# Interleaved stationary columns and a reversed stream in a three-pass matmul kernel

## What is computed

```python
h = rms_norm(x, norm1_g)
z = h @ w_in                                   # pool part, q, k, v, forget gates
x = x + concat([pool_mixer(...), forgetting_attention(...)]) @ w_out
h = rms_norm(x, norm2_g)
q = h @ w_query                                # 8 heads x 2 x 128
# top 16 of 128 keys twice, top 16 of the 256 sums: 128 experts of 16384 for each frame
a = gelu(einsum('thkd,td->thk', expert_u[idx], h))
x = x + einsum('thk,thkd->td', gates * a, expert_v[idx])
```

## Time and profile before

| | us |
|---|---|
| median of 3 runs | 1440.59 (1440.06 to 1440.88) |
| profiled execution, own time | 1441.41 |
| profiled execution, span | 1439.4 |
| PE busy | 1431.6 |
| PE, loads of the stationary | 1277.2 |
| DVE busy | 1133.4 |
| POOL busy | 979.8 |
| ACT busy | 574.4 |

### The profile page before, as it was taken

How to read it: one execution, slowest core, us unless ns; L and a number is a source line. 1 busy time by engine, 2 the same in 40 slices (tenths; PEclk the granted TensorE clock), 3 DMA queues, 4 the chain that set the end, 5 groups by cost and what they waited for, 6 DMA issues and landing times.

```text
span 1439.4 us, 20447 instructions
## 1 busy us (share of the span) xinstructions
PE 1431.6 (99%) x7551; PEld 1277.2 (89%) x7551; DVE 1133.4 (79%) x1876; ACT 574.4 (40%) x799; POOL 979.8 (68%) x533
## 2 busy tenths in 40 slices
PE   9999999999999999999999999999999999999998
PEld 7766798899999999999999999888888888888887
DVE  6678551769999999699999995498777777777775
ACT  5775453333333333444444444333333333333332
POOL 3421544346888788866766675599887888878883
PEclk9999999999999999999999999999999999999999
DMA  6221332235778888989999986998888888888883
GB/s 227 103 89 45 103 113 100 89 100 184 251 262 268 273 272 273 348 281 364 355 360 355 372 296 230 371 383 340 346 346 346 327 326 345 344 341 328 331 302 117
DMA packets 122293, 381.57 MB, mean 265 GB/s; under 512 B 11768, under 2 KB 28280, under 8 KB 122240
## 3 DMA queue, kind: packets, MB, share of 16 engines
q1 hardware_dynamic: 70384, 202.69, 39.5%
q0 software_dynamic: 36864, 134.23, 25.3%
q10 hardware_dynamic: 14992, 44.06, 7.8%
HBM read 336.89 MB, written 44.06 MB: 265 GB/s over the span
## 4 chain that ended last, share of the span: by engine, by line
PE 95%; DVE 2%; DMA 1%; ACT 1%; issue 0%; SPq 0%; DVEq 0%
PE bank L748 28%; PE bank L749 28%; PE bank L750 28%; PE bank L1004 6%; PE bank L936 1%; DMA wf<-a_dram 1%; PE bank L884 1%; PE bank L907 0%; PE wide L896 0%; DVE pad L1235 0%; PE bank L815 0%; PE wide L815 0%; PE bank L826 0%; PE bank L822 0%; PE wide L822 0%
## 5 line engine op out<-in xcount | busy, mean ns | idle before, releaser
L484 POOL TENSOR_TENSOR wl<-raw,wh 128x1024 fp32r<-128x1024 f32 x208 | 507.7, 2442 | 277.7 <-ACT wh L514 275.1
L748 PE MATMUL bank<-hh,wh 128*128 128x384 f32 (+1 forms) x1184 | 416.2, 352 | 0.2 <-DVE hl L1251 0.2
L749 PE MATMUL bank<-hl,wh 128*128 128x384 f32 (+1 forms) x1184 | 406.4, 343 | 0.0
L750 PE MATMUL bank<-hh,wl 128*128 128x384 f32 (+1 forms) x1184 | 406.4, 343 | 0.0
L748 PE MATMUL bank<-wh,Wh 128*128 128x512 f32 x768 | 299.0, 389 | 0.7 <-DVE Wl L1458 0.7
L750 PE MATMUL bank<-wh,Wl 128*128 128x512 f32 x768 | 298.8, 389 | 0.0
L749 PE MATMUL bank<-wl,Wh 128*128 128x512 f32 x768 | 298.8, 389 | 0.0
L514 ACT ACTIVATE wh<-raw 128x1024 fp32r<-128x1024 f32 (+1 forms) x217 | 227.8, 1050 | 141.4 <-PE bank L750 136.4
L748 PEld LDWEIGHTS bank<-hh,wh 128*128 128x128 f32 x1184 | 222.8, 188 | 7.9 <-DVE hl L1251 0.6
L749 PEld LDWEIGHTS bank<-hl,wh 128*128 128x128 f32 x1184 | 222.8, 188 | 7.1 <-issue 0.2
L750 PEld LDWEIGHTS bank<-hh,wl 128*128 128x128 f32 x1184 | 222.3, 188 | 7.6
(11 more groups left out here) (200 smaller groups left out, 1628.6 us busy)
## 6 DMA issues: line engine op xcount, KB each, us to landing
raw<-uT_dram SPq DMA_DIRECT2D x128, 512.0 KB
xraw<-v_dram SPq DMA_DIRECT2D x72, 512.0 KB, 8.5
raw<-v_dram SPq DMA_DIRECT2D x56, 512.0 KB, 9.1
a_dram<-act_a ACTq DMA_DIRECT2D x64, 384.0 KB
wf<-a_dram SPq DMA_DIRECT2D x32, 768.0 KB, 6.8
raw<-wst_dram SPq DMA_DIRECT2D x40, 512.0 KB
gates_dram<-gbuf ACTq DMA_DIRECT2D x32, 512.0 KB
gt<-gates_dram SPq DMA_DIRECT2D x32, 512.0 KB, 4.0
```

Of the source, the lines that this page charges most:

```text
L484: pool.tensor_tensor(wl[:, n % SPLIT, :], raw_of(n), wh[:, n % SPLIT, :].bitcast(F32), ALU.subtract).then_inc(w_lo, 1)
L748: pe.matmul(dst, ah, bh, start=start, stop=False)
L749: pe.matmul(dst, ah, bl, start=False, stop=False)
L750: return pe.matmul(dst, al, bh, start=False, stop=stop)
```

## The change

It has two parts. First, wherever a stationary operand is read from a tile by `project` or `quad`, two neighbouring chunks of the contraction (k = 0 and 1, 2 and 3, ...) are now stored in turn: element 0 of the one, element 0 of the other, element 1 of the one, and so on. A load reads every second column, 128 of 256, and starts at column 0 or 1 of the pair. For the tiles that come from memory the host stores them so (`in_pairs`), with transfers of the same size; for `Wh` and `Wl` ACT and DVE write, and DVE also reads, with a step of two (`by_chunk`). The values and forget tiles stay as they were. Second, in the downs alone the streamed operand and the PSUM bank are both given with a step of -1 (`backwards`), so the columns stream from the last to the first and arrive in their old places. Number, order, waits and sizes of all instructions and transfers are the same on every engine; the two splits L728 and L1458 now have 2 x 2 x 384 instead of 1536 elements a partition.

```diff
+        def in_pairs(w):
+            return w[:, :, :].rearrange("p q t -> p (q t)")
+        def by_chunk(w):
+            return in_pairs(w).rearrange("p (a t c) -> p a c t", a=QUAD // 2, c=2)
+        def pairs_of(w):
+            return w[:, :, :].rearrange("p (a c) t -> p a c t", c=2)
...
-                act.activation(Wh[q % 2][:, :, :], wf[q % LOADS][:, :, :], ACT.Copy).then_inc(W_hi, 1)
+                act.activation(by_chunk(Wh[q % 2]), pairs_of(wf[q % LOADS]), ACT.Copy).then_inc(W_hi, 1)
...
+            def backwards(columns):
+                return columns[:, ::-1]
...
-                    done = three(dst, wh[:, s, k * P:(k + 1) * P], wl[:, s, k * P:(k + 1) * P],
+                    first_column = k // 2 * 2 * P + k % 2
+                    columns = slice(first_column, first_column + 2 * P - 1, 2)
+                    done = three(dst, wh[:, s, columns], wl[:, s, columns],
...
-                            at, d = slice(b * P, (b + 1) * P), slice(half * T, (half + 1) * T)
-                            done = three(bank[2 * b + half][:, :], Wh[s][:, c, at], Wl[s][:, c, at],
-                                         wh[:, static % SPLIT, d], wl[:, static % SPLIT, d], False, end)
+                            first_column = c // 2 * 2 * DT + 2 * P * b + c % 2
+                            at, d = slice(first_column, first_column + 2 * P - 1, 2), slice(half * T, (half + 1) * T)
+                            done = three(backwards(bank[2 * b + half][:, :]), in_pairs(Wh[s])[:, at], in_pairs(Wl[s])[:, at],
+                                         backwards(wh[:, static % SPLIT, d]), backwards(wl[:, static % SPLIT, d]), False, end)
...
-                dve.tensor_tensor(Wl[q % 2][:, :, :], wf[q % LOADS][:, :, :], Wh[q % 2][:, :, :].bitcast(F32),
+                dve.tensor_tensor(by_chunk(Wl[q % 2]), pairs_of(wf[q % LOADS]), by_chunk(Wh[q % 2]).bitcast(F32),
...
+    def in_pairs(chunks):
+        return chunks.reshape(-1, P, KD // 2, 2, P).transpose(0, 1, 2, 4, 3).reshape(-1, P, KD * P)
...
-    wst = np.concatenate([values, column_chunks(forget), qk, cols[0:4], column_chunks(a["wo"][0]),
-                          column_chunks(a["wq"][0])])
+    wst = np.concatenate([values, column_chunks(forget), in_pairs(np.stack(qk)), in_pairs(cols[0:4]),
+                          in_pairs(column_chunks(a["wo"][0])), in_pairs(column_chunks(a["wq"][0]))])
...
-        "uT": a["u"][0].reshape(NCH, P, KD, P).transpose(0, 3, 2, 1).reshape(NCH, P, D),
+        "uT": in_pairs(a["u"][0].reshape(NCH, P, KD, P).transpose(0, 3, 2, 1)),
```

## The result

The changed kernel takes 1468.43 us (1468.32 to 1468.87, 4 runs) against 1440.41 us beside it: 1.0195 times the time, 95% interval 1.0177 to 1.0213. It is 28.0 us slower where 49 us less were forecast, and it lies 8.4 us above the upper end of the range, 1460 us.

What follows compares the result with a forecast made beforehand. TensorE was taken as the bound: number of matmuls times start distance. From the profiled 1441.4 us, 6240 x 8 ns = 49.9 us came off, other terms zero, giving 1391.5, forecast 1391 us; range 1366 to 1460.

Steps and rivals of the forecast that it cites:

- What bounds the kernel: TensorE: time is number of matmuls times start distance; 13.3 ns over the columns' own time on 6240 matmuls, 83.2 us.
- Is the remainder fixed?: Matmuls: the 13.3 ns looked partly like load meeting stream in reading, from five steps at 232 ns, 5 ns more.
- Strided loads: All 6240 matmuls: a load at the stream's pace shortens the wait, 8 ns each, 49.9 us gained; bounds 13.3 either way.
- Backward streaming, inside the 8 ns: Downs, 2304 matmuls: the reversed stream's own cost lies between the same bounds, priced inside the 8 ns.
- L728 and L1458: Strided split on ACT and strided subtraction on DVE, 32 times each: even doubled, covered, so zero on the path.
- The places where a faster TensorE is given back: Retrieval, frames, downs: covered at 8 ns; with the whole remainder gone, 10.8 us given back.
- Rival C: Strided load covers twice the memory, so meetings with the stream cost more: 1457 us at 16 ns, 1524 at 26.7; chance 0.21.
- The signs: Start distances in the trace: near 165 ns in ups and 219 in downs if right; other distances point to rivals.
- the sign of A: Distances of 173.3 and 226.7 ns; rival A: fixed remainder, no change, 1440.6 us, chance 0.14.
- the signs of C: Ups at 180 ns or more; ups above 220 with downs unchanged would mean the load itself is slower.
- The range: Whole kernel: 1366 to 1460 us, taking in the mild end of C and leaving out its larger part, some 0.16.

Runs made afterwards that it cites:

- e7_entry_64: The changed kernel with one more matmul of 64 streamed columns just before the downs: 1461.10 us.
- e8_entry_256: The changed kernel with one more matmul of 256 streamed columns just before the downs: 1460.79 us.

## Why the prediction was wrong

- *What bounds the kernel* was right: PE at 99 to 100%, no wait that counts, time as number times distance. The result can be read off with the same sum to within 1.4 us (28.8 against 27.4), because not all of the 6240 matmuls are settled ones. (The "mean durations (334 and 389 ns)" are medians for the ups: the mean of the earlier trace rows is 342. Nothing hangs on it.)
- *Is the remainder fixed?* The reading of the earlier trace rows was right in kind: how load and stream lie to each other moves the distance, as eight starts show (226.7 to 233.6). What I said of it, that it shows a stall that can grow and not one that can vanish, should have set the sign. No walking form measured is below contiguous, forward and on starts of 128 columns, and that was what the kernel had.
- **The step that failed** is "Strided loads", the gain of 8 ns a matmul in all 6240. It rested on a picture: the stream waits until the load has left a stretch of memory, so a load at the stream's own pace frees it sooner. Two measurements contradict the picture. A load that stays on one column doesn't free the stream (231.8 ns); a load of a quarter of the columns doesn't either (231.9). The stride changed the settled distance by +6.7 ns at 512 columns and by 0 at 384, in place of -8. Between the bounds of -13.3 and +13.3 ns the choice had no row behind it.
- *Backward streaming, inside the 8 ns*: it costs 6.7 ns by itself at 512 columns and 4.4 to 4.7 at 384. On top of a stride of 512 columns it adds nothing in the faster pattern and 3.3 ns in the slower one, which is where the changed kernel ran. Pricing it together with the stride hid that it had a price of its own.
- *L728 and L1458*: priced at nothing on the path, rightly. L728 went from 1473 to 1669 ns, L1458 fell from 2710 to 2422 on average, and PE waits for neither. The places where a faster TensorE is given back were never reached.
- *Rival C* had the sign. Its case of a stall of 16 ns came to 1457 us; nearer still was the 5 ns of the earlier trace rows over all 6240 matmuls, +31 us against the 28.0 measured, but by luck: one family took nothing and another 10 ns. Its mechanism, a cost that doubles with the memory covered, holds in no number: 13.3 became 20.0 in one family and stayed in the other. At 0.21 it had too little, seeing that nothing in the trace showed a form better than the present one.
- *The signs* named beforehand don't have this outcome. The ups stood at 173.3, the sign of A; the 512-column families moved, but up; and with ups unmoved none of the signs of C was there. The forecast's own condition, a fall of at least 3 ns in either family, failed in both.
- *The range* ended at 1460. In the faster pattern the change would have come to about 1461 us, as `e7_entry_64` and `e8_entry_256` did with one matmul more, still a little outside; the last 7.7 us are the pattern, of which nothing before the runs told.
- *The Trainium skill's* two rules, weighed again. The separate read ports (TensorE: Matmul & The Clock Gate, "Step-by-step: what each phase is for"): with a stream that stands still the three forms of the load cost the same (216.8 to 217.1), as the rule has it; with a walking stream a step of 2 in the load alone changes the distance from 226.7 to 233.3, which the rule excludes. Here the measurement decides. "Back-to-back issue gap" of the same page of the Trainium skill, N/2.4 + 2.5 ns, gives an estimate of 215.8 ns for 512 columns: the standing stream comes to within 1.3 ns of it, a walking one with contiguous load was 10.9 above it at its best.

What stays open: which part of the chip makes load and walking stream disturb each other, why 384 columns are spared by the stride and not by the reversal, and what fixes the pattern at the entry. That load and stream meet in memory is the reading that fits best, since a step of two in the load counts with a walking stream (226.7 to 233.3) and not with a standing one (216.9 and 216.8), but the numbers fit no simple count of meetings.

## What to carry to other kernels

In a kernel of back-to-back matmuls, read the distance between starts in the timeline, subtract the columns' own time, and price every edit to an operand's layout by number of matmuls times its change; a few ns are per cents. Keep both operands of such matmuls contiguous, forward and on multiples of 128 four-byte columns unless a run shows better, and measure stride and direction apart. If the distance differs between two kernels with the same instructions there, look at how the stretch is entered, and read more than one stretch before you give a few ns a cause.

## What the runs showed of the hardware that was not expected

- The same instructions can settle at two distances: 233.3 and 236.7 ns with a strided load and a reversed stream, picked at the entry of the stretch and then kept for over 2000 matmuls; in one probe both occur in different rounds of one loop.
- A stream over every second four-byte column runs at half the speed (451.2 ns for 512 columns, against 226.7), while a load over every second column lasts only 6 ns longer (194 against 188). From a step of 3 on the load does slow, from 253 ns to 366 at a step of 12.
- Loading fewer columns made the matmuls stand further apart, 230.0 ns for 64 and 231.9 for 32 against 226.7 for 128.
- Writing the bank backwards costs nothing: 226.7 ns with a forward stream, as before.
